# A second buffer for the scatter-add of the experts' outputs, in a one-core decoder trunk

## The chip, the cores and the metric

The kernel runs on one core of a Trainium2 chip. The metric is the device time of one execution in microseconds, as the median of several runs. The engines are TensorE (PE, with its weight loads PEld), VectorE (DVE), ScalarE (ACT), GpSimd (POOL) and SyncE (SP, which here only issues DMAs); 16 DMA engines move data between HBM and SBUF.

## The reference

One layer of a decoder on 2048 tokens of width 1024, float32, and a final norm. What matters here is the last part:

```
x = x + gate_a * (concat(attention, gated delta rule) @ w_out)
h = rmsnorm(x, moe_norm) * (1 + scale_m) + shift_m
x = x + gate_m * hierarchical_moe(h)   # each token: top-1 group, its top-2 of 8 experts
return rmsnorm(x, final_norm)
```

The experts' part sorts the 4096 pairs of token and expert into blocks of 128 rows, each block of one expert, computes `silu(xb @ w1) * (xb @ w3) @ w2` for each block, scales each row with its gate and adds it to its token's row. Each token gets two such additions, from two different blocks.

## The kernel before, in words

The program is a row of stages, each with a queue of instructions for each engine and a barrier at its end: `modulation`, `projection`, `mix` (attention and delta rule, interleaved), `output`, `routing`, `experts`, `finish`. P = 128, T = 2048 tokens, NT = 16 tiles of tokens, D = 1024.

**mix.** `mix_order()` gives one list of steps that all five engines follow. SP walks it too and issues, step by step, loads of the next tiles (`KS`, `V`), the weights of the modulation (`M`), the store of the delta rule's output (`O2`, L839) and that of the attention's output for one tile of tokens (`A`, L853), for which it waits on `ya_ready` (the tile `attn_y`, written by ScalarE). After the last step it waits for `mod_added` and issues eight small stores of `mod_d` (L856). `mask` is a tile in SBUF of which `mask[:, 0]` is all zeros.

**output.** Writes x after the first sub-layer to the DRAM tensor `x1_d` (`x_d` in the profile, since numbers are left out; its tile is `x_tile`), and the normed rows to `h2_d`. `x1_d` has 128 rows more than tokens, for the empty rows of blocks.

**experts.** A loop over blocks, in pairs (`par` is 0 or 1), as many as routing found. For a block GpSimd gathers 128 rows of `h2_d` (L1781, up to five blocks ahead), TensorE transposes them (L1884), multiplies them with w1 and w3 (L1895), transposes the hidden rows (L1915) and multiplies them with w2 (L1905); VectorE scales the result into `expert_y` (L1863); GpSimd scatters it into `x1_d` with an indirect DMA that adds (L1790). Two blocks can hold rows of the same token, and so each scatter-add waits for the one before it (`y_added[1 - par]`) as well as for the last use of its own `y` slot. SP loads the weights of coming experts into four slots.

**finish.** Per tile of 128 tokens: load of `x1_d` (L1944), Square with row sums on ScalarE (L1971), mean plus epsilon and power -1/2 on GpSimd (L1961, L1963), multiply with that and the final gain on VectorE (L1978), store (L1952). Eight tiles are loaded ahead; each store is followed by the load of the tile eight later. `sp.wait_ge` and the like are waits on semaphores; a DMA adds 16 to its semaphore when it has landed.

Of the kernel before, what the change touches and what calls it, by code (L numbers as in the profile page):

```python
# [22 lines left out]
P = 128  # L23
F32, I32 = mybir.dt.float32, mybir.dt.int32
ALU = mybir.AluOpType
ACT = mybir.ActivationFunctionType
# [3 lines left out]
T, D = 2048, 1024  # L30
# [20 lines left out]
START = 1  # L51
# [623 lines left out]
def mix(nc, m, a_log, dt_bias, w_mod, b_mod):  # L675
# [12 lines left out]
    with nc.cleanup_on_exit(), ExitStack() as ctx:  # L688
# [49 lines left out]
            "av_ready", "ds_ready", "state_ready", "o_ready", "osq_ready", "oss_ready", "o_pow", "yg_ready", "yg_stored"))  # L738
        xw_ready, y_copied, w_ready, u_ready, w_updated, u_updated = (sem(n) for n in (
            "xw_ready", "y_copied", "w_ready", "u_ready", "w_updated", "u_updated"))  # L740
        modw_loaded, mod_ready, mod_added, bias_loaded, mod_stored, bias_zero = (sem(n) for n in (
            "modw_loaded", "mod_ready", "mod_added", "bias_loaded", "mod_stored", "bias_zero"))
        kv_loaded = [sem(f"kv_loaded{s}") for s in range(len(KV) - 1)]
        q_loaded = [sem(f"q_loaded{i}") for i in range(2)]
        s_ready, min_ready, exp_done, t_ready = sem("s_ready"), sem("min_ready"), sem("exp_done"), sem("t_ready")
# [44 lines left out]
        @block.sync  # L790
        def _(sp):
            wait = waiter(sp)

            def load_kv(n):
                t, end = KV[n], KV[n + 1]
                sp.dma_start(kT[:, t:end].rearrange("p t h k -> p t (h k)"),
                             m.kT_d[t * QK:end * QK, :].rearrange("(t p) n -> p t n", p=QK)).then_inc(kv_loaded[n], 16)
                sp.dma_start(v[:, t:end], m.v_d[t * P:end * P, :].rearrange("(t p) n -> p t n", p=P)).then_inc(kv_loaded[n], 16)

            def load_q(i):  # L800
                sp.dma_start(qT[:, i % 2].rearrange("p h t -> p (h t)"), m.qT_d[i * QK:(i + 1) * QK, :]).then_inc(q_loaded[i % 2], 16)

            def load_kq(c):
                sp.dma_start(kq[c % 2][:], m.qkv_d[c:c + 1].rearrange("t p c i -> p (t c) i")).then_inc(kq_loaded[c % 2], 16)

            def load_gate(c):
                sp.dma_start(gate[:].rearrange("p h d -> p (h d)"), m.gate_d[c * P:(c + 1) * P, :]).then_inc(gate_loaded, 16)

            def load_mod(k):
                sp.dma_start(modw[:], w_mod[0, :, 2 * D:].rearrange("(p k) n -> p k n", p=P)[:, k // 2, (k % 2) * 2 * D:(k % 2 + 1) * 2 * D]  # L810
                             ).then_inc(modw_loaded, 16)

            load_q(0)
            load_kv(0)
            sp.dma_start(alog[:], a_log[0:1, :].partition_broadcast(P)).then_inc(rows_loaded, 16)
            sp.dma_start(dtb[:], dt_bias[0:1, :].partition_broadcast(P)).then_inc(rows_loaded, 16)
            load_q(1)
            load_kv(1)
            load_kq(0)
            load_kq(1)  # L820
            load_kv(2)
            load_gate(0)
            sp.wait_ge(bias_zero, 1)
            for r in range(8):
                sp.dma_start(mod_sum[32 * (r % 4):32 * (r % 4) + 1, r // 4], b_mod[0:1, 2 * D + r * 512:2 * D + (r + 1) * 512]).then_inc(bias_loaded, 16)
            load_mod(0)
            sp.wait_ge(mask_made, 1)
            for step in order:
                kind, n = step[0], step[1]
                if kind == "KS" and n + 2 < NT:  # L830
                    wait(ks_ready, n + 1)
                    load_kq(n + 2)
                elif kind == "M":
                    wait(mod_ready, n + 1)
                    if n + 1 < NMK:
                        load_mod(n + 1)
                elif kind == "O2":
                    wait(yg_ready, n + 1)
                    sp.dma_start(m.y_d[n * P:(n + 1) * P, AH * DV:], gate[:].rearrange("p h d -> p (h d)")).then_inc(yg_stored, 16)  # L839
                    if n + 1 < NT:  # L840
                        wait(yg_stored, 16 * (n + 1))
                        load_gate(n + 1)
                elif kind == "V" and n in last_j:
                    i = last_j.index(n)
                    if i + 2 < NT:
                        wait(s_ready, 2 * (n + 1))
                        load_q(i + 2)
                    for s in range(3, len(KV) - 1):
                        if i == max(0, KV[s] - 5):
                            load_kv(s)  # L850
                elif kind == "A":
                    wait(ya_ready, n + 1)
                    sp.dma_start(m.y_d[n * P:(n + 1) * P, 0:AH * DV], ya[:]).then_inc(ya_stored, 16)  # L853
            sp.wait_ge(mod_added, NMK)
            for r in range(8):
                sp.dma_start(m.mod_d[0:1, r * 512:(r + 1) * 512], mod_sum[32 * (r % 4):32 * (r % 4) + 1, r // 4]).then_inc(mod_stored, 16)  # L856
            sp.wait_ge(yg_stored, 16 * NT)
            sp.wait_ge(ya_stored, 16 * NT)
            sp.wait_ge(mod_stored, 16 * 8)
# [840 lines left out]
def experts(nc, m, w1, w3, w2):  # L1700
# [6 lines left out]
    with nc.cleanup_on_exit(), ExitStack() as ctx:  # L1707
# [64 lines left out]
        def _(pool):  # L1772
# [11 lines left out]
            def add(b, par):  # L1784
                wait(y_added[par], (b - par) * 8 - START)
                pool.tensor_copy(row[par][:], m.slot_row[:, ds(b, 1)]).then_inc(row_copied, 1)
                wait(row_copied, b + 1)
                wait(y_ready, b * 2 + 2)
                wait(y_added[1 - par], (b + par) * 8 - START)
                pool.indirect_dma_start(m.x1_d, bass.IndirectOffsetOnAxis(ap=row[par][:, 0:1], axis=0), y[:, par], None,  # L1790
                                        compute_op=ALU.add).then_inc(y_added[par], 16)

            n = pairs(pool)
# [135 lines left out]
def finish(nc, m, final_norm, out):  # L1929

    with nc.cleanup_on_exit(), ExitStack() as ctx:  # L1931
        sb = lambda n, s, d=F32: ctx.enter_context(nc.sbuf_tensor(n, s, d))
        sem = nc.alloc_semaphore
        GROUP = 4
        fgain, xa, junk = sb("final_gain", [P, D]), sb("x2", [P, NT, D]), sb("junk7", [P, 2, D])
        ss, ms, rs = sb("x2_sumsq", [P, NT]), sb("x2_meansq", [P, NT]), sb("x2_rstd", [P, NT])
        gain_loaded, squared, powed, out_ready, stored = (sem(n) for n in ("gain_loaded", "squared7", "powed7", "out_ready7", "stored7"))
        x_loaded = [sem(f"x_loaded7_{i}") for i in range(NT)]
        block = ctx.enter_context(nc.Block())

        @block.sync
        def _(sp):
            def load(t):
                sp.dma_start(xa[:, t], m.x1_d[t * P:(t + 1) * P, :]).then_inc(x_loaded[t], 16)  # L1944

            load(0)
            sp.dma_start(fgain[:], final_norm.rearrange("(a n) -> a n", a=1).partition_broadcast(P)).then_inc(gain_loaded, 16)  # L1947
            for t in range(1, 2 * GROUP):
                load(t)
            for t in range(NT):  # L1950
                sp.wait_ge(out_ready, t + 1)
                sp.dma_start(out[0, t * P:(t + 1) * P, :], xa[:, t]).then_inc(stored, 16)  # L1952
                if t + 2 * GROUP < NT:
                    load(t + 2 * GROUP)
            sp.wait_ge(stored, 16 * NT)

        @block.gpsimd
        def _(pool):
            for t in range(NT):
                pool.wait_ge(squared, t + 1)  # L1960
                pool.tensor_scalar(ms[:, t:t + 1], ss[:, t:t + 1], 1.0 / D, EPS, ALU.mult, ALU.add).then_inc(powed, 1)  # L1961
                pool.wait_ge(powed, 2 * t + 1)
                pool.tensor_tensor(rs[:, t:t + 1], ms[:, t:t + 1], m.half_pow[:, 0:1], ALU.pow).then_inc(powed, 1)  # L1963

        @block.scalar
        def _(act):
            for t in range(NT):
                act.wait_ge(x_loaded[t], 16)
                if t >= 2:
                    act.wait_ge(squared, t - 1)  # L1970
                act.activation(junk[:, t % 2], xa[:, t], ACT.Square, accum_out=ss[:, t:t + 1]).then_inc(squared, 1)  # L1971

        @block.vector
        def _(dve):
            dve.wait_ge(gain_loaded, 16)
            for t in range(NT):
                dve.wait_ge(powed, 2 * t + 2)
                dve.scalar_tensor_tensor(out=xa[:, t], in0=xa[:, t], scalar=rs[:, t:t + 1], in1=fgain[:],  # L1978
                                         op0=ALU.mult, op1=ALU.mult).then_inc(out_ready, 1)


def trunk(nc, x, c, positions, w_mod, b_mod, attn_norm, w_in, q_norm, w_uq, kv_norm, w_ukv, conv_w, a_log, dt_bias,
          mla_out_norm, gdn_out_norm, w_out, moe_norm, w_route_group, b_route_group, w_route_expert, b_route_expert,
          w1, w3, w2, final_norm, out):
    with ExitStack() as ctx:
# [15 lines left out]
        with (nc.sbuf_tensor("rope_sin", [P, NT * HALF], F32) as m.sin, nc.sbuf_tensor("rope_cos", [P, NT * HALF], F32) as m.cos,  # L2001
              nc.sbuf_tensor("w_in_sb", [P, ND, DIN], F32) as m.win):
            modulation(nc, m, c, positions, w_mod, b_mod, attn_norm, w_in)
            projection(nc, m, x, q_norm, w_uq, kv_norm, w_ukv, conv_w)
        m.mod_d = dram("mod_d", [1, 4 * D])
        mix(nc, m, a_log, dt_bias, w_mod, b_mod)
        m.mod_rows = sb("mod_rows", [P, 4, D])
# [42 lines left out]
```

## Time and profile before

| | |
|---|---|
| median of 3 runs | 2830.23 us (2829.51 to 2832.22) |
| profiled execution | 2830.23 us, span 2828.5 us |
| busy share of the span | PE 90%, DVE 41%, ACT 30%, POOL 19% |
| first and last block's scatter-add issued | 2252.4 us, 2770.8 us |
| finish, first load issued to end of span | 2782.9 us to 2828.5 us |
| moved by DMA in the whole span | 331.29 MB |

Times in the profile are microseconds from the start of the span, one duration of an instruction may be given in ns. PE, PEld, DVE, ACT, POOL and SPq name the engine; "out<-in" are the tiles written and read, with numbers in their names left out. An arrow `<-` in a wait points to what ended it. The granted clock of TensorE is given as a share of full speed.

### The profile page before, as it was taken

To read this page: it belongs to the slowest core of one execution; us is meant where nothing else is said; L and a number is where in the kernel's file an instruction comes from. 1 tells how busy PE (TensorE), PEld (TensorE's weight loads), DVE (VectorE), ACT (ScalarE), POOL (GpSimd) and SP (SyncE) were. 2 spreads that over 40 slices of the span, in tenths; PEclk is the share of its full clock that TensorE was granted. 3 is DMA by queue.
4 is the path that set the end of the run, shared out by engine and by line. 5 is a ranking of instruction groups with operands and counts; after the bars stand their busy time and mean duration, and the time that the engine had idled before them with its cause. 6 is when DMAs were issued, how large, how long until landed. Compare 5 with 4: busy or idle time off the path is not lost. (4 is left out here: it accounts for less than half of the span.)

```text
span 2828.5 us, 37391 instructions
## 1 busy us (share of the span) xinstructions
PE 2532.6 (90%) x12276; PEld 1561.5 (55%) x12277; DVE 1148.8 (41%) x2333; ACT 854.8 (30%) x2023; POOL 546.1 (19%) x755
## 2 busy tenths in 40 slices
PE   7699999999959999999999999659995699999991
PEld 7344444444437777776777777535553444444440
DVE  0234334333335666666666666512224322222223
ACT  0224335242344444444444444311110011111112
POOL 0110000000021221222212122012331122222224
PEclk9999999999979999999999999879997799999995
DMA  7212112121162113111111110183331187999787
GB/s 263 75 49 73 54 54 71 44 67 36 50 177 77 54 44 96 55 51 44 44 38 45 61 49 27 61 314 119 119 119 52 52 267 230 280 298 321 224 263 268
DMA packets 174366, 331.29 MB, mean 117 GB/s; under 512 B 19840, under 2 KB 110976, under 8 KB 172048
## 3 DMA queue, kind: packets, MB, share of 16 engines
q1 hardware_dynamic: 160272, 279.09, 29.2%
q0 software_dynamic: 13952, 50.36, 7.3%
q8 instruction: 83, 1.36, 0.2%
q14 instruction: 59, 0.48, 0.1%
HBM read 238.17 MB, written 91.24 MB: 116 GB/s over the span
## 5 line engine op out<-in xcount | busy, mean ns | idle before, releaser
L604 PE MATMUL pV<-h_transposed,w_in_sb 128*128 128x512 f32 x768 | 337.6, 593 | 1.6 <-ACT h_transposed L399 1.6
L1895 PE MATMUL hidden_ps<-w,h_rowsT 128*128 x752 | 331.6, 594 | 1.1 <-SPq L1767 1.1
L978 ACT ACTIVATE probs<-scores,neg_max 128x512 f32<-128x512 f32 (+3 forms) x320 | 199.3, 623 | 382.6 <-DVE neg_max L1124 259.0
L1267 PE MATMUL scores<-keys,queries 96*128 96x512 f32 (+3 forms) x640 | 289.0, 533 | 14.1 <-DMA values<-v_d 14.1
L1895 PEld LDWEIGHTS hidden_ps<-w,h_rowsT 128*128 128x128 f32 x752 | 143.5, 191 | 181.4 <-issue 181.3
L604 PEld LDWEIGHTS pV<-h_transposed,w_in_sb 128*128 128x128 f32 x768 | 144.8, 190 | 174.6 <-issue 169.6
L1484 PE MATMUL out_ps<-w_out_sb,yT 128*128 128x512 f32 x512 | 225.4, 599 | 2.2 <-DVE yT L1457 2.2
L899 POOL TENSOR_TENSOR X_transposed<-A_transposed,level_masks 128x512 f32<-128x512 f32 x112 | 140.9, 1270 | 408.7 <-DVE A_transposed L1049 195.8
L1272 PE MATMUL bank<-ident,probs 128*128 128x128 f32 x1088 | 178.7, 280 | 3.6 <-ACT probs L978 2.7
L1124 DVE TENSOR_REDUCE neg_max<-scores 128x1 f32<-128x512 f32 x192 | 132.4, 690 | 104.8 <-PE scores L1267 103.8
L1905 PE MATMUL expert_ps<-w_sb,hiddenT 128*128 x368 | 169.8, 604 | 0.0
L1272 PEld LDWEIGHTS bank<-ident,probs 128*128 128x128 f32 x1088 | 127.0, 141 | 74.3 <-issue 69.3
L1282 PE MATMUL outT_ps<-probs_T,values 128*64 128x128 f32 x2176 | 155.5, 281 | 11.7 <-issue 5.9
L1484 PEld LDWEIGHTS out_ps<-w_out_sb,yT 128*128 128x128 f32 x512 | 96.8, 192 | 118.5 <-issue 115.7
L1825 ACT ACTIVATE silu_gate<-hidden_ps 128x256 f32<-128x256 f32 x47 | 18.0, 383 | 455.5 <-PE hidden_ps L1895 455.5
L1282 PEld LDWEIGHTS outT_ps<-probs_T,values 128*64 128x64 f32 x2176 | 116.9, 137 | 68.2 <-issue 55.6
L1854 DVE TENSOR_TENSOR hidden<-silu_gate,hidden_ps 128x256 f32<-128x256 f32 x47 | 19.8, 422 | 277.4 <-ACT silu_gate L1825 277.4
L522 DVE TENSOR_SCALAR conv_acc<-conv_in,conv_taps 128x512 f32<-128x512 f32 x48 | 23.7, 493 | 243.5 <-ACT conv_in L441 243.5
L1863 DVE SCALAR_TENSOR_TENSOR expert_y<-expert_ps,slot_gate,mod_rows 128x512 f32<-128x512 f32 x92 | 64.8, 746 | 133.1 <-PE expert_ps L1905 133.1
L1267 PEld LDWEIGHTS scores<-keys,queries 96*128 96x128 f32 x640 | 99.7, 194 | 27.2 <-issue 25.8
L560 PE MATMUL pG<-w_in_sb,h_transposed 128*128 128x512 f32 x256 | 112.5, 593 | 0.0
L1220 PE MATMUL bank<-W_all,X_transposed 128*128 128x128 f32 x768 | 104.4, 280 | 7.2 <-ACT W_all L955 4.8
(332 smaller groups left out, 3893.4 us busy)
## 6 DMA issues: line engine op xcount, KB each, us to landing
w<-in_w_dram SPq DMA_DIRECT2D x64, 1024.0 KB, 10.8
w_sb<-in_w_dram SPq DMA_DIRECT2D x32, 1024.0 KB, 14.5
w_mod_rows<-in_w_mod_dram SPq DMA_DIRECT2D x16, 1024.0 KB, 4.9
kqv<-qkv_d SPq DMA_DIRECT2D x16, 768.0 KB, 4.2
mod_w<-in_w_mod_dram SPq DMA_DIRECT2D x2, 4096.0 KB, 21.7
x_in<-in_x_dram SPq DMA_DIRECT2D x16, 512.0 KB, 3.5
qkv_d<-l_out SPq DMA_DIRECT2D x32, 256.0 KB, 2.3
y_in<-y_d SPq DMA_DIRECT2D x16, 512.0 KB, 4.4
```

Source lines behind the costliest of these rows:

```text
L560: last = pe.matmul(pG[:], hT[:, n // ST % 2, k, n % ST * P:(n % ST + 1) * P], win[:, k, GATE0:], start=(k == 0), stop=(k == ND - 1))
L604: last = pe.matmul(pV[n % 2][:], win[:, k, QKV0 + c * P:QKV0 + (c + 1) * P], hT[:, s % 2, k, :], start=(k == 0), stop=(k == ND - 1))
L899: pool.tensor_tensor(xt[:, t % 3], lt[:], masks[:, lv].unsqueeze(1).to_broadcast([P, GH, P]), ALU.mult).then_inc(xt_ready, 1)
L978: act.activation(prob[:, e, 0:w].rearrange("p t k -> p (t k)"), pS[e][:, 0:w * P], ACT.Exp, scale=-1.0, bias=nmin[:, i % 2, h, b:b + 1], a ...
L1124: dve.tensor_reduce(nmin[:, i % 2, h, b:b + 1], pS[e][:, 0:w], AX.X, ALU.min).then_inc(min_ready, 1)
L1220: last = pe.matmul(bank[b0][:, h], xt[:, (LV * n + lv) % 3, h], W[:, h], start=True, stop=True)
L1267: pe.matmul(pS[e][:, 0:w * P], qT[:, i % 2, h], kT[:, 4 * b:4 * b + w, h, :], start=True, stop=True).then_inc(s_ready, 1)
L1272: last = pe.transpose(bank[b0][:, t], prob[:, e, t], m.ident[:])
L1282: last = pe.matmul(pO[64 * e:64 * e + 64, n % 4], v[:, 4 * b + t, h * DV:(h + 1) * DV], probT[:, n % 2, e, t], start=(t == 0), stop=(t == ...
L1484: last = pe.matmul(pX[:, half], yT[par][:, k], wo[:, k, half * 512:(half + 1) * 512], start=(k == 0), stop=(k == ND - 1))
L1895: last = pe.matmul(pH[par][:], xT[par][:, k], m.w13[:, ds(slot, 1), k].rearrange("p s n -> p (s n)"), start=(k == 0), stop=(k == ND - 1))
L1905: last = pe.matmul(pY[:, half], hT[par][:, k], m.w2b[:, ds(slot, 1), k, half * 512:(half + 1) * 512].rearrange("p s n -> p (s n)"), start= ...
```

## The change

The additions of even blocks go to `x1_d` as before, those of odd blocks to a second DRAM tensor `y2_d` of the same size. A scatter-add now waits only for the one two blocks before it. `y2_d` is set to zero in the mix: at each `A` step SP issues, ahead of its wait for `ya_ready`, one store of 128 rows of zeros, read from `mask[:, 0]` eight times over in pieces of 512 bytes, and one more at the first `A` step, for the extra rows; SP waits for all 17 before the `mod_d` stores. The finish loads a tile from both tensors, VectorE adds them into `x2` ahead of the Square, and the result goes to a tile of its own, `ob`. Five tiles are loaded ahead, `x2` and `ob` have four slots each, and VectorE adds tile t+1 before it multiplies tile t.

```diff
@@ mix, block.sync
                 elif kind == "A":
+                    sp.dma_start(m.y2_d[n * P:(n + 1) * P, :].rearrange("p (c n) -> p c n", n=P), mask[:, 0].unsqueeze(1).to_broadcast([P, D // P, P])
+                                 ).then_inc(zeros_stored, 16)
+                    if n == 0:
+                        sp.dma_start(m.y2_d[T:, :].rearrange("p (c n) -> p c n", n=P), mask[:, 0].unsqueeze(1).to_broadcast([P, D // P, P])
+                                     ).then_inc(zeros_stored, 16)
                     wait(ya_ready, n + 1)
...
             sp.wait_ge(mod_added, NMK)
+            sp.wait_ge(zeros_stored, 16 * 17)
@@ experts, block.gpsimd, add
                 wait(y_ready, b * 2 + 2)
-                wait(y_added[1 - par], (b + par) * 8 - START)
-                pool.indirect_dma_start(m.x1_d, bass.IndirectOffsetOnAxis(ap=row[par][:, 0:1], axis=0), y[:, par], None,
+                pool.indirect_dma_start((m.x1_d, m.y2_d)[par], bass.IndirectOffsetOnAxis(ap=row[par][:, 0:1], axis=0), y[:, par], None,
                                         compute_op=ALU.add).then_inc(y_added[par], 16)
@@ finish, block.sync (DEPTH = 5)
-            def load(t):
+            for t in range(DEPTH):
                 sp.dma_start(xa[:, t], m.x1_d[t * P:(t + 1) * P, :]).then_inc(x_loaded[t], 16)
-
-            load(0)
-            sp.dma_start(fgain[:], final_norm.rearrange("(a n) -> a n", a=1).partition_broadcast(P)).then_inc(gain_loaded, 16)
-            for t in range(1, 2 * GROUP):
-                load(t)
+                sp.dma_start(xb[:, t], m.y2_d[t * P:(t + 1) * P, :]).then_inc(x_loaded[t], 16)
+                if t == 0:
+                    sp.dma_start(fgain[:], final_norm.rearrange("(a n) -> a n", a=1).partition_broadcast(P)).then_inc(gain_loaded, 16)
             for t in range(NT):
                 sp.wait_ge(out_ready, t + 1)
-                sp.dma_start(out[0, t * P:(t + 1) * P, :], xa[:, t]).then_inc(stored, 16)
-                if t + 2 * GROUP < NT:
-                    load(t + 2 * GROUP)
+                sp.dma_start(out[0, t * P:(t + 1) * P, :], ob[:, t % 4]).then_inc(stored[t % 4], 16)
+                if t + DEPTH < NT:
+                    sp.dma_start(xa[:, t % DEPTH], m.x1_d[(t + DEPTH) * P:(t + DEPTH + 1) * P, :]).then_inc(x_loaded[t % DEPTH], 16)
+                    sp.dma_start(xb[:, t % DEPTH], m.y2_d[(t + DEPTH) * P:(t + DEPTH + 1) * P, :]).then_inc(x_loaded[t % DEPTH], 16)
@@ finish, block.scalar
-                act.wait_ge(x_loaded[t], 16)
+                act.wait_ge(x2_ready, t + 1)
@@ finish, block.vector
+            def summed(t):
+                dve.wait_ge(x_loaded[t % DEPTH], 32 * (t // DEPTH + 1))
+                if t >= 4:
+                    dve.wait_ge(out_ready, t - 3)
+                dve.tensor_tensor(x2[:, t % 4], xa[:, t % DEPTH], xb[:, t % DEPTH], ALU.add).then_inc(x2_ready, 1)
+
+            summed(0)
             for t in range(NT):
+                if t + 1 < NT:
+                    summed(t + 1)
                 dve.wait_ge(powed, 2 * t + 2)
-                dve.scalar_tensor_tensor(out=xa[:, t], in0=xa[:, t], scalar=rs[:, t:t + 1], in1=fgain[:],
+                if t >= 4:
+                    dve.wait_ge(stored[t % 4], 16 * (t // 4))
+                dve.scalar_tensor_tensor(out=ob[:, t % 4], in0=x2[:, t % 4], scalar=rs[:, t:t + 1], in1=fgain[:],
                                          op0=ALU.mult, op1=ALU.mult).then_inc(out_ready, 1)
```

## Rows read from the trace of the kernel before

**Rows 1.** Stretches: busy time of each engine, granted clock, DMA share, GB/s.

```profile
core 0: us, PE busy (x) PEld busy (x) DVE busy (x) ACT busy (x) POOL busy (x), PEclk, DMA share, GB/s
2240.00:2770.00 530.00, 527.16 (x1561) 258.42 (x1559) 116.05 (x184) 56.68 (x138) 136.41 (x182) 1.00 0.85 256
2790.00:2826.00 36.00, 0.00 (x0) 0.00 (x0) 19.26 (x15) 17.24 (x30) 25.26 (x30) 0.50 1.03 419
15.00:20.00 5.00, 1.73 (x9) 1.76 (x9) 4.55 (x15) 0.42 (x1) 0.00 (x0) 1.00 1.03 414
1870.00:1880.00 10.00, 10.00 (x24) 4.45 (x23) 0.00 (x0) 0.00 (x0) 0.00 (x0) 0.96 1.07 364
```

**Rows 2.** Waits, 2230 to 2790 us: us in total, times, longest.

```profile
POOL x_d L1790 <- DVE expert_y L1863: 168.5, 42, 4.1
...
POOL x_d L1790 <- DMA x_d<-expert_y,out_row: 8.6, 2, 4.6
...
PE hidden_ps L1895 <- SPq L1767: 1.1, 1, 1.1
```

**Rows 3.** Timeline: start, us, engine, line, operation; in brackets the idle time before.

```profile
2745.12 7.03 PE L1895 MATMUL hidden_ps<-w,h_rowsT 128*128 x16
...
2756.61 7.03 PE L1895 MATMUL hidden_ps<-w,h_rowsT 128*128 x16
...
2759.27 1.60 POOL L1790 DMA_INDIRECT x_d<-expert_y,out_row  x1 [3.98 <-DVE expert_y L1863]
...
2770.81 1.60 POOL L1790 DMA_INDIRECT x_d<-expert_y,out_row  x1 [4.04 <-DVE expert_y L1863]
```

**Rows 4.** The 46 scatter-adds of L1790, from issue to landing.

```profile
DMA to landing us min/median/max: 6.0/8.8/10.7
```

**Rows 5.** Timeline of the finish.

```profile
2782.87 0.35 SPq L1944 DMA_DIRECT2D x<-x_d  x1
...
2800.20 1.06 ACT L1971 ACTIVATE junk<-x 128x1024 f32<-128x1024 f32 x1 [1.34 <-DMA x<-x_d]
...
2817.64 1.06 ACT L1971 ACTIVATE junk<-x 128x1024 f32<-128x1024 f32 x1 [1.35 <-DMA x<-x_d]
```

**Rows 6.** DMA issues: count, KB each, median us from issue to landing.

```profile
qkv_d<-l_out SPq DMA_DIRECT2D x32, 256.0 KB, 2.3
...
x_d<-x_tile SPq DMA_DIRECT2D x16, 512.0 KB, 2.6
...
x<-x_d SPq DMA_DIRECT2D x16, 512.0 KB, 9.6
out_dram<-x SPq DMA_DIRECT2D x16, 512.0 KB, 9.1
```

**Rows 7.** Waits of SP's queue, 700 to 2200 us.

```profile
SPq L853 <- ACT attn_y L999: 189.7, 15, 35.2
```

**Rows 8.** Waits of TensorE for a DMA, 700 to 1840 us.

```profile
PE scores L1267 <- DMA values<-v_d: 14.1, 1, 14.1
```

**Rows 9.** Timeline of the end of the mix.

```profile
1816.85 0.68 DVE L1111 TENSOR_TENSOR mod_sum<-mod_sum,bank 128x512 f32<-128x512 f32 x1
...
1826.35 2.55 SPq L856 DMA_DIRECT2D mod_d<-mod_sum  x8
```

**Rows 10.** Groups of VectorE's instructions by form: busy us, mean ns.

```profile
L1978 DVE SCALAR_TENSOR_TENSOR x<-x,x_rstd,final_gain 128x1024 f32<-128x1024 f32 x16 | 20.5, 1284 | 31.1 <-DMA final_gain<-in_final_norm_dram 18.8 <-POOL x_rstd L1963 12.3
...
L1675 DVE TENSOR_TENSOR blk_hot<-blk_hot,gates 128x1024 f32<-128x1024 f32 x2 | 2.5, 1226 | 0.1
```

**Rows 11.** Timeline of the finish, its first tiles.

```profile
2786.09 1.06 ACT L1971 ACTIVATE junk<-x 128x1024 f32<-128x1024 f32 x1 [20.73 <-DMA x<-x_d]
...
2787.33 0.19 POOL L1961 TENSOR_SCALAR x_meansq<-x_sumsq 128x1 f32<-128x1 f32 x1 [14.92 <-ACT junk L1971]
2787.61 0.58 POOL L1963 TENSOR_TENSOR x_rstd<-x_meansq,half_pow 128x1 f32<-128x1 f32 x1
...
2794.22 1.28 POOL L1961 TENSOR_SCALAR x_meansq<-x_sumsq 128x1 f32<-128x1 f32 x1
```

More of the change, by code:

```diff
@@ L740, in mix @@
             "xw_ready", "y_copied", "w_ready", "u_ready", "w_updated", "u_updated"))
-        modw_loaded, mod_ready, mod_added, bias_loaded, mod_stored, bias_zero = (sem(n) for n in (
-            "modw_loaded", "mod_ready", "mod_added", "bias_loaded", "mod_stored", "bias_zero"))
+        modw_loaded, mod_ready, mod_added, bias_loaded, mod_stored, bias_zero, zeros_stored = (sem(n) for n in (
+            "modw_loaded", "mod_ready", "mod_added", "bias_loaded", "mod_stored", "bias_zero", "zeros_stored"))
         kv_loaded = [sem(f"kv_loaded{s}") for s in range(len(KV) - 1)]
@@ L1933, in finish @@
         sem = nc.alloc_semaphore
-        GROUP = 4
-        fgain, xa, junk = sb("final_gain", [P, D]), sb("x2", [P, NT, D]), sb("junk7", [P, 2, D])
+        DEPTH = 5
+        fgain = sb("final_gain", [P, D])
+        xa, xb = sb("sum_a", [P, DEPTH, D]), sb("sum_b", [P, DEPTH, D])
+        x2, ob, junk = sb("x2", [P, 4, D]), sb("out_tile", [P, 4, D]), sb("junk7", [P, 2, D])
         ss, ms, rs = sb("x2_sumsq", [P, NT]), sb("x2_meansq", [P, NT]), sb("x2_rstd", [P, NT])
-        gain_loaded, squared, powed, out_ready, stored = (sem(n) for n in ("gain_loaded", "squared7", "powed7", "out_ready7", "stored7"))
-        x_loaded = [sem(f"x_loaded7_{i}") for i in range(NT)]
+        gain_loaded = sem("gain_loaded")
+        x_loaded = [sem(f"x_loaded7_{i}") for i in range(DEPTH)]
+        x2_ready, squared, powed, out_ready = sem("x2_ready"), sem("squared7"), sem("powed7"), sem("out_ready7")
+        stored = [sem(f"stored7_{i}") for i in range(4)]
         block = ctx.enter_context(nc.Block())
@@ L1942, in _ @@
         def _(sp):
-            def load(t):
+            for t in range(DEPTH):
                 sp.dma_start(xa[:, t], m.x1_d[t * P:(t + 1) * P, :]).then_inc(x_loaded[t], 16)
-            load(0)
-            sp.dma_start(fgain[:], final_norm.rearrange("(a n) -> a n", a=1).partition_broadcast(P)).then_inc(gain_loaded, 16)
-            for t in range(1, 2 * GROUP):
-                load(t)
+                sp.dma_start(xb[:, t], m.y2_d[t * P:(t + 1) * P, :]).then_inc(x_loaded[t], 16)
+                if t == 0:
+                    sp.dma_start(fgain[:], final_norm.rearrange("(a n) -> a n", a=1).partition_broadcast(P)).then_inc(gain_loaded, 16)
             for t in range(NT):
                 sp.wait_ge(out_ready, t + 1)
-                sp.dma_start(out[0, t * P:(t + 1) * P, :], xa[:, t]).then_inc(stored, 16)
-                if t + 2 * GROUP < NT:
-                    load(t + 2 * GROUP)
-            sp.wait_ge(stored, 16 * NT)
+                sp.dma_start(out[0, t * P:(t + 1) * P, :], ob[:, t % 4]).then_inc(stored[t % 4], 16)
+                if t + DEPTH < NT:
+                    sp.dma_start(xa[:, t % DEPTH], m.x1_d[(t + DEPTH) * P:(t + DEPTH + 1) * P, :]).then_inc(x_loaded[t % DEPTH], 16)
+                    sp.dma_start(xb[:, t % DEPTH], m.y2_d[(t + DEPTH) * P:(t + DEPTH + 1) * P, :]).then_inc(x_loaded[t % DEPTH], 16)
+            for i in range(4):
+                sp.wait_ge(stored[i], 16 * NT // 4)
         @block.gpsimd
@@ L1967, in _ @@
             for t in range(NT):
-                act.wait_ge(x_loaded[t], 16)
+                act.wait_ge(x2_ready, t + 1)
                 if t >= 2:
                     act.wait_ge(squared, t - 1)
-                act.activation(junk[:, t % 2], xa[:, t], ACT.Square, accum_out=ss[:, t:t + 1]).then_inc(squared, 1)
+                act.activation(junk[:, t % 2], x2[:, t % 4], ACT.Square, accum_out=ss[:, t:t + 1]).then_inc(squared, 1)
         @block.vector
@@ L2004, in trunk @@
             projection(nc, m, x, q_norm, w_uq, kv_norm, w_ukv, conv_w)
+        m.y2_d = dram("y2_d", [T + P, D])
         m.mod_d = dram("mod_d", [1, 4 * D])
```

## The prediction

> **What bounds the kernel now.** I read the table of stretches first, because the change touches three stages and each has its own limit. In the experts' stage TensorE is busy 527.2 of 530 us at the full granted clock, 1.00 [rows 1]; in the finish it does nothing, and the DMA engines are busy all the time, share 1.03 at 419 GB/s from 2790 to 2826 us [rows 1]. So the experts are bound by TensorE and the finish by transfers. Two limits, and the change trades something in the one against something in the other.
>
> Next the waits of the experts' stage. TensorE's only wait in it is 1.1 us, for the weights [rows 2]. The scatter-add (L1790) waits 42 times for VectorE's rows, 168.5 us in all, and only twice, 8.6 us, for the transfer of the scatter before it [rows 2]. The timeline says why: one block follows the other every 11.49 us (2756.61 - 2745.12), set by TensorE, and the scatters are issued in the same step, 2759.27, 2770.81 [rows 3]. A scatter lands 8.8 us after its issue in the median, 10.7 at most [rows 4]: it is down before the next one is ready.
>
> Last the finish. From 2800.20 to 2817.64 a Square starts every 2.491 us (17.44 / 7), each after the landing of its load [rows 5]. One load and one store, 512 KB each, go in this time, so one transfer costs 1.246 us (524,288 bytes / 1.246 us = 421 GB/s, what the table of stretches shows too). The queue is deep: a load takes 9.6 us to land, a store 9.1 [rows 6], where a store of this size alone takes 2.6 us [rows 6]. The stage has 16 loads, the gain row and 16 stores, 33 transfers x 1.246 = 41.1 us; from the first issue (2782.87 [rows 5]) to the end of the span (2828.5) are 45.6 us, so 4.5 us are start, gain row and last landing. The engines are not the limit: from 2790 to 2826 us VectorE is busy 19.3 of 36 us, ScalarE 17.2, GpSimd 25.3 [rows 1].
>
> **The change part by part.**
>
> *The wait taken out of the scatter.* It has cost GpSimd 8.6 us [rows 2], none of which reached TensorE: what TensorE waited for in the whole stage is 1.1 us, for weights. Behind the scatter in GpSimd's queue stands the gather for a later block, and TensorE never waited for a gather. The gain lies between 0 and 1.1 us; I take 0. The last scatter, issued at 2770.81, waits for VectorE and not for its forerunner, needs at least 6.0 us to land [rows 4], and the first load of the finish follows at 2782.87 [rows 5]; both buffers have to be down before that, and nothing of these 12 us depends on which of them the last scatter goes to. 0 again.
>
> *The zero stores in the mix.* 17 transfers of 512 KB in pieces of 512 B. Nearest row: 256 KB in pieces of that size land in 2.3 us [rows 6]; 256 KB more at 1.246 / 2 makes about 3 us. The issue itself is some 0.36 us of SP's time. SP issues each where it otherwise waits for attn_y: it waited there 15 times for 189.7 us [rows 7], 12.6 us each, so the issue hides behind that wait. TensorE waits for a DMA once in this stage, at its beginning, 14.1 us [rows 8], before the first "A" step. The new wait for the zeros stands ahead of the eight mod_d stores, and behind those the loads of the next stage. In the order the last "A" step comes behind the last "M" step, whose sum VectorE has started at 1816.85; the mod_d stores are issued from 1826.35 on [rows 9], so the last zeros have over 9 us for their 3. I take 0. If the cover were gone: 17 x 0.36 = 6 us for the issues, 17 x 3 = 51 us if each transfer stood in the way of one that TensorE needs; no wait in the trace makes the latter likely.
>
> *The finish.* 16 loads of the second buffer are added to a queue that is never empty: 33 transfers become 49, 16 x 1.246 = **+19.9 us**. For this the queue has to stay full with 5 tiles in flight. At the start 11 transfers are issued at once, 11 x 1.246 = 13.7 us of work; with the 4.5 us around them the queue runs dry at 18.2 us. The first output needs the second tile's pair too (five transfers, 4.5 + 6.2 = 10.7 us), since VectorE adds tile t+1 ahead of multiplying tile t, and then add and multiply, 2.6 us more: 13.3 us, in time. Later on a tile takes 3 transfers, 3.74 us; its output comes about 3.74 + 2.6 = 6.3 us after its pair has landed, in which 1.7 of the 5 pairs have been used up, so about three wait in the queue. No gap. VectorE's new waits, for the store of tile t-4 and for x2 of tile t-4, are not last: that store is queued ahead of the pair t+1, and the output of t waits for that pair anyway.
>
> The engines: the new add is [128 x 1024] f32 on VectorE; the nearest row is a tensor_tensor of this shape, 1.226 us [rows 10]. Per tile VectorE has 1.226 + 1.284 = 2.5 us [rows 10]. GpSimd's mean takes 0.19 us alone (2787.33) but 1.28 us when it meets VectorE's multiply (2794.22 [rows 11]): it is held until that is over. If the add holds it as well, the loop is multiply, add, mean, power, 1.28 + 1.23 + 0.19 + 0.55 = 3.25 us and four hand-overs of some 0.07, 3.5 us, still under 3.74. The Trainium skill (SBUF — State Buffer, Who interferes with whom) says that a tensor_tensor with both inputs in SBUF does contend with GpSimd's reads. By it the loop is the 3.5 us just worked out, without it 2.5 to 3.3; the sum stays the same by either, only the margin shrinks to 0.2 us.
>
> The tail grows. After the last load lands, five stores are left; the queue needs 5 x 1.246 = 6.2 us for them, but the last one has to wait for its tile: add 1.23, from the start of Square to the end of the power 2.10 (2786.09 to 2787.61 + 0.58 [rows 11]), multiply 1.28, hand-overs 0.2, then 2.6 us for a store alone = 7.4 us. That is 1.2 us over the queue's time; since before, eight stores took 10.9 us (2817.64 to 2828.5) where 8 x 1.246 = 10.0, part of it is there already, and I take +1.0 us.
>
> **The sum.** 0 + 0 + 19.9 + 1.0 = +20.9 us. The profiled execution has a span of 2828.5 us and a time of 2830.23, 1.7 us around it, and it is also the median of the three runs. 2830.2 + 20.9 = **2851.1 us**.
>
> Of the rate, the Trainium skill (DMA: Bandwidth & Descriptors, Where 436 GB/s comes from) says that transfers between HBM and SBUF are bound by HBM's share of a core, about 358 GB/s. By that rate 16 x 524,288 bytes would cost 23.4 us (an estimate from that page) in place of 19.9. The trace has 419 GB/s over 36 us of this stage [rows 1], so the rule doesn't hold here for one load to one store; for two loads to one store no row tells.
>
> **The rivals.**
>
> 1. *Loads are slower than stores when there are more of them.* For: stretches that are nearly all loads show 364 GB/s (1870 to 1880 [rows 1]); against: another shows 414 (15 to 20 [rows 1]), and the slow one reads the experts' weights in 1 KB pieces while these are 4 KB rows. At 364 a load takes 1.44 us; 32 loads x 0.194 = 6.2 us more, **2857 us**. Chance 0.10. [...]
> 2. *The zero stores are not free.* If SP reaches its "A" steps late, the issues cost up to 6 us, **2857 us**; a loss beyond that needs a transfer of which the trace shows no wait. Chance 0.04.
> 3. *The engines become the bound of the finish.* Against: 3.5 against 3.74 us. It decides from a loop over 3.74 us. With no overlap of tiles at all a tile takes 1.23 + 1.25 + 1.28 + 0.55 + 1.28 and 0.4 of hand-overs = 6.0 us, 16 x 6.0 + about 8 = 104 us against 45.6, **2888 us**; VectorE adds tile t+1 before it multiplies tile t, which speaks against it. Chance 0.03.
> 4. *The other side: the scatters run freer and the experts' stage gets shorter.* The place is the block step of 11.49 us. It decides only if 46 blocks save over 20.9 + 5.7 us, 0.58 us each, that is, if TensorE had hidden waits in its step (the ends of its matmuls are modelled). Then the step would be 10.9 us and the time **2824 us**. Against: TensorE shows 1.1 us of waits in the stage. Chance 0.02.
> 5. *The second buffer's loads are hidden,* so that nothing changes: it needs spare DMA time in the finish; share 1.03 [rows 1] leaves none. With 0.02 for it, **2831 us**.
>
> **How the numbers follow.** The forecast keeps 0.79. 0.2% is 5.7 us, about what a measurement of this kernel can tell from no change. Faster by more: rival 4, 0.02. Within: rival 5, 0.02. Slower: the rest, 0.96. The range: from below, 16 x 1.246 = 19.9 with no longer tail and the full 1.1 us back from the experts' stage, 2849, and 2 us for a better rate in the start, 2847; from above the bounds of rivals 1 and 2, 2857, with the tail's uncertainty 2859. It leaves out rivals 3 to 5 and the far ends.
>
> **What the changed profile would show.** In the finish: 49 transfers, DMA share near 1.03 and about 420 GB/s for some 56 us, one Square every 3.7 us, each waiting for VectorE's add, which waits for a DMA. A step of 3.9 us at a lower rate means rival 1; a full share gone and VectorE or GpSimd busy without a break means rival 3. In the experts' stage: TensorE 527 of 530 us as before, the step 11.49, and no wait of L1790 for a DMA. In the mix: SP's waits for attn_y shorter by 0.4 us each, TensorE's waits as before, the zeros landing in about 3 us. The prediction is wrong if the first load of the finish is not issued at about 2783 us (mix or experts moved) or if the finish is not 66.5 us long.

## The result, and the profile after

| | before | changed |
|---|---|---|
| median | 2829.93 us (2829.51 to 2832.22, 4 runs) | 2850.62 us (2846.66 to 2852.78, 4 runs) |
| profiled execution: span | 2828.5 us | 2849.1 us |
| finish: first load issued | 2782.87 us | 2781.62 us |
| finish: from there to the end of the span | 45.6 us | 67.5 us |

The ratio is 1.0074, with a 95% interval of 1.006 to 1.0086: slower by 0.7%, 20.7 us between the medians, 20.6 between the spans. In the two profiled executions the finish takes 21.9 us more, and all that lies ahead of it 1.25 us less.

In the profile `y2_d` is `y_d` (numbers are left out), the tiles loaded from the two tensors are `sum_a` and `sum_b`, their sum is `x`, the tile that is stored `out_tile`, and `mask` is `diag_mask`. The table of stretches, changed kernel, the same columns as in [rows 1]:

```profile
core 0: us, PE busy (x) PEld busy (x) DVE busy (x) ACT busy (x) POOL busy (x), PEclk, DMA share, GB/s
2240.00:2770.00 530.00, 526.94 (x1561) 258.08 (x1559) 116.09 (x184) 56.73 (x138) 137.44 (x183) 1.00 0.86 256
2806.00:2840.00 34.00, 0.00 (x0) 0.00 (x0) 22.08 (x19) 10.35 (x18) 7.16 (x20) 0.50 1.03 419
```

The experts' stage has the same busy TensorE as in [rows 1]. The finish has the same DMA share and the same 419 GB/s, although two loads now go with each store. Nothing moves faster or slower there; there is more to move.

The waits, changed kernel, 2230 to 2790 us (as [rows 2]):

```profile
POOL x_d L1795 <- DVE expert_y L1868: 89.5, 23, 4.0
POOL y_d L1795 <- DVE expert_y L1868: 85.1, 22, 3.9
...
POOL y_d L1795 <- issue: 4.8, 1, 4.8
```

The first and the last of them in the timeline, changed kernel:

```profile
2252.32 1.64 POOL L1795 DMA_INDIRECT x_d<-expert_y,out_row  x1 [4.00 <-DVE expert_y L1868]
...
2769.31 1.60 POOL L1795 DMA_INDIRECT y_d<-expert_y,out_row  x1 [3.86 <-DVE expert_y L1868]
```

The scatter-adds (L1795 now) go 23 to each tensor and no longer wait for a transfer. They wait for VectorE instead, 174.6 us where it was 168.5: most of what the edit took away has gone into the wait that was there anyway, for the blocks come no faster. From the issue of the first scatter-add to that of the last are 517.0 us (2769.31 - 2252.32), where before has 518.4; the kernels e1 and e3 below, which keep the removed wait, have 517.1.

The timeline of the finish, changed kernel: first the start, then one tile in its steady part, then the tail.

```profile
2789.18 1.22 DVE L1990 TENSOR_TENSOR x<-sum_a,sum_b 128x1024 f32<-128x1024 f32 x1 [20.69 <-DMA final_gain<-in_final_norm_dram]
...
2797.61 1.22 DVE L1990 TENSOR_TENSOR x<-sum_a,sum_b 128x1024 f32<-128x1024 f32 x1
2797.83 1.41 POOL L1972 TENSOR_TENSOR x_rstd<-x_meansq,half_pow 128x1 f32<-128x1 f32 x1
...
2800.47 1.22 DVE L1990 TENSOR_TENSOR x<-sum_a,sum_b 128x1024 f32<-128x1024 f32 x1
...
2806.98 1.23 DVE L1990 TENSOR_TENSOR x<-sum_a,sum_b 128x1024 f32<-128x1024 f32 x1 [0.70 <-DMA sum_b<-y_d]
...
2809.75 0.55 POOL L1972 TENSOR_TENSOR x_rstd<-x_meansq,half_pow 128x1 f32<-128x1 f32 x1
...
2840.86 1.23 DVE L1990 TENSOR_TENSOR x<-sum_a,sum_b 128x1024 f32<-128x1024 f32 x1 [1.35 <-DMA sum_b<-y_d]
...
2844.21 1.28 DVE L1999 SCALAR_TENSOR_TENSOR out_tile<-x,x_rstd,final_gain 128x1024 f32<-128x1024 f32 x1 [0.93 <-POOL x_rstd L1972]
```

Two regimes are to be seen. The first tiles find their loads landed, and their adds follow each other in 2.86 us (2797.61 to 2800.47) with no wait in brackets: the engines set the pace. From 2806.98 to 2840.86 are nine tiles, 3.76 us each, and every add waits for a load of `y_d`: the transfers set it (against 2.49 in [rows 5]).

DMA issues, changed kernel (as [rows 6]):

```profile
y_d<-diag_mask SPq DMA_DIRECT2D x17, 512.0 KB, 6.0
...
sum_a<-x_d SPq DMA_DIRECT2D x16, 512.0 KB, 10.3
sum_b<-y_d SPq DMA_DIRECT2D x16, 512.0 KB, 11.1
out_dram<-out_tile SPq DMA_DIRECT2D x16, 512.0 KB, 9.0
```

The chain that ended last, changed kernel, links from its end (start, us, what):

```profile
2829.06 11.78 DMA sum_b<-y_d
2840.86 1.24 DVE x L1990
2842.12 1.06 ACT junk L1980
...
2843.35 0.19 POOL x_meansq L1970
...
2844.21 1.28 DVE out_tile L1999
```

Add, Square, mean, power and multiply follow the last landing, and only then can the last store go.

### The profile page after: what moved, and what is told of

It is laid out like the page before. It is cut to its first block and busy times, and to the rows that moved or that the text cites. A ratio compares the mean times of both kernels' runs of the same rounds, so it can differ in the third digit from the quotient of the medians.

```text
span 2849.1 us, 37400 instructions
## 1 busy us (share of the span) xinstructions
PE 2533.8 (89%) x12276; PEld 1561.0 (55%) x12277; DVE 1167.4 (41%) x2349; ACT 855.6 (30%) x2023; POOL 539.1 (19%) x755
## 5 line engine op out<-in xcount | busy, mean ns | idle before, releaser
L1273 PE MATMUL scores<-keys,queries 96*128 96x512 f32 (+3 forms) x640 | 289.2, 534 | 13.3 <-DMA values<-v_d 13.3
```

What stands on the lines that cost most here:

```text
L1273: pe.matmul(pS[e][:, 0:w * P], qT[:, i % 2, h], kT[:, 4 * b:4 * b + w, h, :], start=True, stop=True).then_inc(s_ready, 1)
```

## The experiments

The theory: the loss is the second tensor's 16 loads in a stage that is bound by its transfers, plus a longer tail; the split scatter gains nothing and the zeros cost nothing. The rivals are those of the prediction. The kernel before was run beside each of the three groups of experiments; its medians were 2828.91 (e1 to e4), 2829.5 (e5, e6, e9, e10) and 2828.01 us (e8). Single executions scatter by some us, most of it ahead of the finish (its first load is issued between 2778.6 and 2783.6 us in the profiles), so besides the medians I compare the length of the finish, from its first load's issue to the end of the span. The changed kernel has 67.5 us, before 45.6; the three profiles of kernels whose finish does the same work (changed, e3, e5) have 67.4 to 68.0, so a difference of half a microsecond in one profile tells nothing.

| kernel | median, us | ratio to before (95%) | finish, us |
|---|---|---|---|
| e1: zeros alone | 2829.01 | 0.9999 (0.999 to 1.0008) | 45.7 |
| e2: zeros and split scatter | 2828.79 | 0.9997 (0.9988 to 1.0006) | 45.6 |
| e3: zeros and new finish | 2850.43 | 1.0079 (1.0065 to 1.0092) | 68.0 |
| e4: second load halved | 2842.75 | 1.0046 (1.0032 to 1.006) | 60.0 |
| e5: three times the zeros | 2851.4 | 1.0084 (1.0069 to 1.01) | 67.4 |
| e6: 3 tiles in flight | 2868.36 | 1.0136 (1.0121 to 1.0152) | 85.4 |
| e9: loads without the add | 2849.11 | 1.0075 (1.0061 to 1.0089) | 66.7 |
| e10: add without the loads | 2842.46 | 1.0046 (1.0033 to 1.006) | 58.2 |
| e8: before, gain loaded early | 2827.81 | 1.0 (0.9991 to 1.0009) | 45.4 |

**The parts one by one: e1, e2, e3.**

e1, on the kernel before:

```diff
                 elif kind == "A":
+                    sp.dma_start(m.y2_d[n * P:(n + 1) * P, :]..., mask[:, 0]...).then_inc(zeros_stored, 16)
...
                     wait(ya_ready, n + 1)
...
+            sp.wait_ge(zeros_stored, 16 * 17)
```

> The kernel before plus the 17 zero stores in the mix, and nothing else. My theory (the zeros hide behind SP's wait for attn_y, and no engine waits for the transfers they share the queue with): 2830 us, within 1 us of before. Rival 2 (the zeros are not free): 6 us for the issues if SP comes late, 2836, and up to 17 x 6.0 us (the landing that the changed kernel's profile shows) if each stands in another transfer's way.

Measured 2829.01 against 2828.91 us. No cost is to be seen; by the interval it would be at most 2.3 us. TensorE's only wait for a DMA in the mix is still the one at its beginning, and from the Matmul behind that wait to the first store of `mod_d` are 1013.3 us, where before has 1012.9, e8 (no zeros either) 1012.6, and e5 with three times the zeros 1013.0. The other kernels with 17 zero stores scatter about this, 1010.1 to 1016.0. The profile of e1 also has no wait of TensorE in the experts' stage, although its scatter-adds still wait for each other: the 1.1 us of [rows 2] come and go between executions and are no effect of the wait that was removed.

e2, on e1:

```diff
-                wait(y_added[1 - par], (b + par) * 8 - START)
-                pool.indirect_dma_start(m.x1_d, ...
+                pool.indirect_dma_start((m.x1_d, m.y2_d)[par], ...
```

> The zero stores and the scatter-add split over two tensors, without the wait between neighbours, with the finish of before. The finish reads the first tensor alone, so the additions of the odd blocks are left out of the output. My theory (TensorE sets the block's step, the wait cost it nothing): 2829 to 2830 us, at most the 1.1 us better that TensorE waited for weights. Rival 4 (the scatters run freer and the experts' stage gets shorter by many us): well below 2825.

Measured 2828.79, and 2829.01 for e1: the split gains nothing that can be measured. The profiles say it more closely. From the first scatter-add's issue to the last one's are 516.9 us in e2; in the kernels that keep the wait these are 517.1 us (e1, e3 and e8), so the wait was worth 0.1 to 0.2 us. Before itself has 518.4, and its profile is the one with TensorE's 1.1 us wait for weights.

e3, on the changed kernel:

```diff
-                pool.indirect_dma_start((m.x1_d, m.y2_d)[par], ...
+                wait(y_added[1 - par], (b + par) * 8 - START)
+                pool.indirect_dma_start(m.x1_d, ...
```

> The zero stores and the new finish with its second load and add, but all scatter-adds go to the first tensor again, with the wait for the one before. My theory (all of the loss is the finish): 2851 us, as the changed kernel, at most 1 us more. If the split scatter were a part of the loss or of a gain, this would be away from it by that part.

Measured 2850.43, as expected. The finish alone carries the loss. Its loads read the second tensor as zeros here and as sums in the changed kernel; the step is the same.

**Bytes or engines: e4, e9, e10.**

e4, on the changed kernel, in all loads of `xb` and in the add:

```diff
-                sp.dma_start(xb[:, t], m.y2_d[t * P:(t + 1) * P, :]).then_inc(x_loaded[t], 16)
+                sp.dma_start(xb[:, t, 0:D // 2], m.y2_d[t * P:(t + 1) * P, 0:D // 2]).then_inc(x_loaded[t], 16)
...
-                dve.tensor_tensor(x2[:, t % 4], xa[:, t % DEPTH], xb[:, t % DEPTH], ALU.add).then_inc(x2_ready, 1)
+                dve.tensor_tensor(x2..., xa..., xb[:, t % DEPTH, 0:D // 2].unsqueeze(1).to_broadcast([P, 2, D // 2]), ALU.add).then_inc(x2_ready, 1)
```

> The changed kernel with a second load of half the width (256 KB per tile in place of 512, that half added to both halves of x); the right half of the second tensor is left out and the left half added twice. The instructions are as many as in the changed kernel. My theory (bytes at 1.246 us per 512 KB): 16 x 0.623 = 10.0 us less, 2841 us, if the tile's step of 3.1 us stays above the engines' loop, which the changed profile shows at 2.86 us where no transfer is waited for. Rival 3 or a cost per instruction or per transfer (issue, landing, add): no more than a few us less, 2848.

Measured 2842.75: of the two it is nearer to bytes, but 7.5 us of finish came back, not 10. Where a part of the rest went shows in its table of stretches (e4; columns as above):

```profile
2794.00:2806.00 12.00, 0.00 (x0) 0.00 (x0) 10.23 (x9) 4.60 (x8) 8.22 (x9) 0.50 1.01 367
2810.00:2820.00 10.00, 0.00 (x0) 0.00 (x0) 8.26 (x7) 3.81 (x8) 5.47 (x8) 0.50 1.03 416
```

From 2794 to 2806 the rate is 367 GB/s at a DMA share of 1.01, and only later is it 416: by bytes, that is 1.4 us lost. The first store is issued 12.8 us after the first load (2780.99 to 2793.76), while the loads issued at the start are worth only 8.5 transfers of 1.246 us, 10.6 us (an estimate), so the queue is nearly empty there. That this lowers the rate is argued, not shown by a run; the other 1.1 us stay open. The adds follow each other in 2.86 us with their loads landed until 2813.85, and wait for loads in a step of 3.15 us from 2817.02 on. So here the two limits are close, which led to the next pair.

e9, on the changed kernel:

```diff
-                dve.tensor_tensor(x2[:, t % 4], xa[:, t % DEPTH], xb[:, t % DEPTH], ALU.add).then_inc(x2_ready, 1)
+                dve.sem_inc(x2_ready, 1)
...
-                act.activation(junk[:, t % 2], x2[:, t % 4], ACT.Square, accum_out=ss[:, t:t + 1]).then_inc(squared, 1)
+                act.wait_ge(x_loaded[t % DEPTH], 32 * (t // DEPTH + 1))
+                act.activation(junk[:, t % 2], xa[:, t % DEPTH], ACT.Square, accum_out=ss[:, t:t + 1]).then_inc(squared, 1)
...
-                dve.scalar_tensor_tensor(out=ob[:, t % 4], in0=x2[:, t % 4], ...
+                dve.scalar_tensor_tensor(out=ob[:, t % 4], in0=xa[:, t % DEPTH], ...
```

> The changed kernel without its add: both loads run as they do, but Square and multiply read the first tensor's tile and the second is left out of the output. My theory (bytes set the finish in all but its tail): the tail alone gets shorter by the add, about 1 us, 2850 us. Rival 3 (VectorE's add, which holds up GpSimd, is a part of the loss): several us less than 2850.

Measured 2849.11, and a finish 0.8 us shorter than the changed kernel's: of the size of the add's 1.22 us in the tail, and nothing else.

e10, on the changed kernel (`xb[:, 0]` is loaded once, all other loads of the second tensor are gone):

```diff
-                sp.dma_start(xb[:, t], m.y2_d[t * P:(t + 1) * P, :]).then_inc(x_loaded[t], 16)
                 if t == 0:
+                    sp.dma_start(xb[:, 0], m.y2_d[0:P, :]).then_inc(xb_loaded, 16)
...
-                dve.wait_ge(x_loaded[t % DEPTH], 32 * (t // DEPTH + 1))
+                dve.wait_ge(x_loaded[t % DEPTH], 16 * (t // DEPTH + 1))
...
-                dve.tensor_tensor(x2[:, t % 4], xa[:, t % DEPTH], xb[:, t % DEPTH], ALU.add).then_inc(x2_ready, 1)
+                dve.tensor_tensor(x2[:, t % 4], xa[:, t % DEPTH], xb[:, 0], ALU.add).then_inc(x2_ready, 1)
```

> The other half: the add runs in each tile, but the second tensor is loaded once (its first tile, added to each one; the rest of it is left out), so that 34 transfers are left of 49. By bytes alone it would be 15 x 1.25 = 18.7 us less, 2832 us. The changed kernel's profile shows that the engines' loop is 2.86 us a tile where no load is waited for, over the 2.49 us that load and store of a tile take: with the first multiply 11.5 us after the first issue, 15 steps of 2.86, and 4 us for multiply and store, the finish takes 58 us in place of 45.6 and the time is 2842. So I expect 2842: the engines hide under the bytes, but would cost over half of the loss by themselves. Rival (pure bytes): 2832.

Measured 2842.46 us, against 2842 by the engines' loop and 2832 by bytes. Its timeline and its table of stretches:

```profile
2800.86 1.22 DVE L1990 TENSOR_TENSOR x<-sum_a,sum_b 128x1024 f32<-128x1024 f32 x1
...
2801.08 1.41 POOL L1971 TENSOR_TENSOR x_rstd<-x_meansq,half_pow 128x1 f32<-128x1 f32 x1
...
2802.52 1.28 DVE L1999 SCALAR_TENSOR_TENSOR out_tile<-x,x_rstd,final_gain 128x1024 f32<-128x1024 f32 x1 [0.44 <-POOL x_rstd L1971]
...
2803.72 1.22 DVE L1990 TENSOR_TENSOR x<-sum_a,sum_b 128x1024 f32<-128x1024 f32 x1
...
2795.00:2835.00 40.00, 0.00 (x0) 0.00 (x0) 33.82 (x29) 16.10 (x28) 26.76 (x29) 0.50 0.89 328
```

The step is 2.86 us from the third add to the last, and of the 16 adds one alone waits for a load, 0.4 us: the engines set the pace. The DMA share is down to 0.89, with a rate of 328 GB/s (0.95 and 346 up to 2826, while loads are still issued). GpSimd's power takes 0.55 us when VectorE is idle, and 1.41 us beside the add: it ends 0.4 us after the add does, and VectorE's multiply waits for it. The loop is multiply, add, rest of the power: 1.2 + 1.22 + 0.44. That is the rule of the Trainium skill (SBUF — State Buffer, Who interferes with whom) that a tensor_tensor with both inputs in SBUF contends with GpSimd's reads; the traces of the changed kernel and of e10 agree.

The bytes without the add (e9) lengthen the finish by 21.1 us, the add and the new order of the finish with one load of the second tensor in place of 16 (e10) by 12.6, both together by 21.9. They lie beside each other, and the larger one counts, but for the tail.

**Is the queue kept full by 5 tiles: e6.**

```diff
-        DEPTH = 5
+        DEPTH = 3
```

> The changed kernel with 3 tiles in flight in place of 5. My theory says that 5 keep the queue full; with 3 a pair is issued only when the queue is nearly empty. An output comes 2.4 us after the landing of the next tile's pair, then three issues and three transfers with some 2 us of latency, 5.8 us, for two tiles on: 4.15 us per tile in place of 3.76, and a gap of 2 us at the start: 5 + 2 = 7 us more, 2858 us, and a DMA share under 1. Rival (the depth plays no role, the rate is all): 2851.

Measured 2868.36: the direction is right and the size is not, 17.9 us of finish more in place of 7. Stretches, then VectorE's waits for the second tensor's loads and the time of these loads to landing:

```profile
2800.00:2840.00 40.00, 0.00 (x0) 0.00 (x0) 19.44 (x17) 9.20 (x16) 5.92 (x16) 0.50 0.93 339
2821.00:2822.00 1.00, 0.00 (x0) 0.00 (x0) 1.00 (x1) 0.00 (x0) 0.00 (x0) 0.50 1.05 299
2822.00:2823.00 1.00, 0.00 (x0) 0.00 (x0) 1.00 (x2) 0.88 (x1) 0.00 (x0) 0.50 1.10 348
...
  DMA sum_b<-y_d: 33.4, 14
...
DMA to landing us min/median/max: 4.1/6.5/10.2
```

The share is 0.93 and the rate 339 GB/s, not 1.03 and 419. So the queue runs low between tiles, but that is not all: the share fell by a tenth, the rate by a fifth, and in single microseconds with a share of 1.05 and 1.10 (2821 to 2823) it is 299 and 348 GB/s. The rate fell even where the DMA engines show as busy, which nothing in my sum had. The adds are 4.77 us apart (2802.67 to 2859.9, 12 steps) where I had 4.15. Of the 17.9 us, 3.9 are lost up to the fourth add and 14.0 from there to the last; the tail is the same. A pair's second load took 6.5 us to land in the median, 1.5 us over what I had allowed from its issue on; which part of the latency grew isn't settled. With 5 tiles there is no such gap: the changed kernel's first store is issued 13.2 us after its first load (2781.62 to 2794.86), and in stretches of 4 us no rate from 2789.6 to 2841.6 is under 414 GB/s.

**Do the zeros hide with a margin: e5.**

```diff
-                    sp.dma_start(m.y2_d[n * P:(n + 1) * P, :]..., mask[:, 0]...).then_inc(zeros_stored, 16)
+                    for y_zero in (m.y2_d, m.y3_d, m.y4_d):
+                        sp.dma_start(y_zero[n * P:(n + 1) * P, :]..., mask[:, 0]...).then_inc(zeros_stored, 16)
...
-            sp.wait_ge(zeros_stored, 16 * 17)
+            sp.wait_ge(zeros_stored, 16 * 49)
```

> The changed kernel with three times the zero stores: 49 in place of 17, the additional ones into two tensors that nobody reads. My theory (SP's wait for attn_y, some 12 us per tile, and an idle queue cover them): 2851 us as the changed kernel; the last zeros, three in a row at about 6 us for the first and less for the others, should still be down before the mod_d stores, 10 us later, or delay them by 1 to 4 us. Rival 2 (zeros cost something each that the noise hid): three times that, visible from 2 us on.

Measured 2851.4, the finish 67.4 us. Three times the zeros change nothing that can be told: single issues take up to 7.3 us of SP's time, and SP's wait for attn_y shrinks from 188.9 to 125.2 us and absorbs them. The stretch of the mix measured under e1 is 1013.0 us long, as with 17 zero stores or with none.

**A version that might beat both: e8,** on the kernel before:

```diff
@@ experts, block.sync
+            sp.dma_start(m.fgain[:], final_norm.rearrange("(a n) -> a n", a=1).partition_broadcast(P)).then_inc(m.gain_loaded, 16)
             with sp.Fori(1, NE // WSLOTS) as i:
@@ finish, block.sync
-            sp.dma_start(fgain[:], final_norm.rearrange("(a n) -> a n", a=1).partition_broadcast(P)).then_inc(gain_loaded, 16)
```

> The kernel before with the load of the final gain moved from the finish to the start of the experts' stage, into a tile that is allocated there: a version that might beat both, since the finish is bound by its transfers. My theory: one transfer of 1.25 us less, and up to 1.3 us more since the gain row, read again and again for 128 partitions, moves at 217 GB/s in the profile where other transfers have 420: the finish 1.3 to 2.5 us shorter, 2827 us against 2829.5 of before, at the edge of what the runs can tell; the profile shows it. Rival (the new transfer among the weights costs TensorE a wait in the experts' stage): 0 to 2 us the other way.

Measured 2827.81 against 2828.01 us, no difference; the finish is 45.4 us long, 0.2 us less, not 1.3 to 2.5. The profile of e8 has a dip after its start that before doesn't have:

```profile
2783.57:2787.57 4.00, 0.00 (x0) 0.00 (x0) 1.71 (x2) 2.64 (x6) 2.34 (x4) 0.50 1.00 376
2787.57:2791.57 4.00, 0.00 (x0) 0.00 (x0) 2.57 (x3) 3.61 (x8) 3.42 (x5) 0.50 0.97 322
2791.57:2795.57 4.00, 0.00 (x0) 0.00 (x0) 2.57 (x3) 2.30 (x4) 3.66 (x5) 0.50 1.02 414
```

Before has 417 GB/s in the third 4 us of its finish, e8 322: what one transfer less gave is lost again there. Why the rate dips stays open. The 217 GB/s of my expectation was the rate of a stretch at the start of the stage, and taking the gain row out of it did not bring the difference back. No version tried beats the kernel before.

## Why the prediction was right

*The wait gains nothing.* Right. e2 against e1 shows it, and the length of the experts' stage, 516.9 against 517.1 us. GpSimd's queue had slack behind TensorE's step, and the freed time went into the wait for VectorE.

*The zeros cost nothing.* Right in the sum, wrong in a size: the term "256 KB more at 1.246 / 2 makes about 3 us" was 3 us, and a zero store took 6.0 us to land in the median; its issue 0.53 us in place of 0.36. The last one was issued at 1815.09 and the mod_d stores at 1826.22, so 11 us covered the 6. e5 shows that three times as much is covered too. The sign "SP's waits for attn_y shorter by 0.4 us each" can't be read: 188.9 us in 16 waits against 189.7 in 15, since the profile of before puts one more such wait, 26.2 us, down to another line.

*16 transfers of 1.246 us, 19.9 us.* Right: the rate is the same 419 GB/s with two loads to a store, which speaks against rival 1, and the DMA share of 1.03 left no room for rival 5. The queue stayed full: the first store came 13.2 us after the first load, where 13.3 was forecast. e9 has all of it without the add.

*The tail, +1.0 us.* Right as a difference. From the last load's landing (2840.86) to the end of the span are 8.2 us, against 5 x 1.246 = 6.2 for the queue alone, 2.0 over; before the same excess was 0.9, so 1.1 more. The chain itself was put at 7.4 us and took 8.2: its last piece, from the end of the last multiply (2845.49) to the end of the span, took 3.6 us in place of the 2.6 of a store alone. e9, without the add, gets 0.8 back.

*What the sum missed.* From the first issue to the last landing are 59.2 us with 44 transfers, 4.4 us over 44 x 1.246 = 54.8; before it was 34.8 us with 25 transfers, 3.6 over. These 0.8 us are not in the sum: 0.2 of them are the nine steps of 3.76 us in place of 3.74, and where the rest comes from isn't settled. And 1.25 us went the other way ahead of the finish: the first scatter-add is issued at the same time (2252.37 and 2252.32), the last one 1.5 us earlier, and 1.1 us of it is TensorE's wait for weights, which is in the profile of before and not in that of the changed kernel. No edit did that, since e1 and e3, with the old wait, are as short. 19.9 + 1.1 + 0.8 - 1.25 = 20.6 us. So the mechanism is right, and that the total came within 0.5 us of the forecast (2850.62 against 2851.1) is luck in part: the finish was to be 66.5 us long and was 67.5, and a chance difference of about the same size ahead of it took this away again.

*The engines (rival 3).* Not the bound of the stage, as predicted, but my loop was wrong in its form: I added mean and power to multiply and add and had 3.5 us; the mean runs while VectorE works or waits, and only 0.44 us of the power stick out, 2.86 us. The margin to 3.74 was 0.9 us and not 0.2. For the first tiles, whose loads lie ready, this loop was indeed the pace, which no part of the prediction had said; the queue stayed full meanwhile (414 GB/s and more).

## What to carry to other kernels

Before a wait is bought off with a second buffer, look at what the waiting engine does next: if it only waits longer for the engine that sets the pace, nothing is gained, while the merging of the buffers is paid for in full where it falls, here in a stage at DMA share 1.03, as bytes over rate. In a stage bound by transfers, count the transfers at the measured time of one, check that the queue stays full, and add the chain from the last landing to the last store. Work that lies under the transfers (the add, 12.6 us by itself) isn't free in itself, and comes out as soon as the bytes are taken away.

## What the runs showed of the hardware that was not expected

- GpSimd's [128 x 1] power took 0.55 us beside an idle VectorE and 1.41 us when VectorE's add of two tiles in SBUF ran beside it.
- A store of 512 KB in pieces of 512 B, read from one 512 B piece per partition again and again, took 6.0 us to land in the median (3.5 at least), where a store of 4 KB rows took 2.6 [rows 6]. The two were issued in different stages, and no run separates the pieces from the other transfers about them.
- Two loads to one store ran at 419 GB/s, as one to one did.
- A DMA share near 1 did not mean the full rate: 416 to 419 GB/s at 1.03 with many transfers queued, but 367 at 1.01 (e4, 2794 to 2806) and 322 at 0.97 (e8). The cause is not shown.
- Executions of the same kernel lie up to 9 us apart (before: 2825.21 to 2834.24 us in 21 executions), with the mean granted clock lower in the longer ones, 0.957 in the longest and 0.962 in the shortest. A difference of 2 us is read from the length of a stage, not from the totals.
